# The start of a two-block transformer kernel reworked, one attention half reordered, and products of zeros put between hand-overs

## The reference

```
h += [stick_breaking(z), mlstm(z), spatial_gating(z)] @ w_out    # z = rms_norm(h, g1) @ w_in
h += moe(rms_norm(h, g2))                     # router: 4 groups of 8 experts, top 2
h += sigmoid(rms_norm(h) @ ple_gate) * (p @ ple_proj);   h = rms_norm(h)
h += (B * conv3(C * V)) @ sc_w_out            # [B|C|V] = rmsnorm(h) @ sc_w_in
h += conv_ffn(rmsnorm(h))                     # silu(g) * u @ w_down, 2816 wide
h += moba_attention(rmsnorm(h))               # 16 heads of 64, rope, causal softmax
h += conv_ffn(rmsnorm(h));  return rmsnorm(h)
```

## Time and profile before

| | |
|---|---|
| time, 3 runs | median 1277.6 us (1277.28 to 1283.98) |
| the profiled execution | 1279.39 us |
| its span | 1277.6 us |
| TensorE busy | 1174.7 us, 92% |
| VectorE busy | 864.5 us, 68% |
| ScalarE busy | 698.0 us, 55% |
| GpSimd busy | 124.3 us, 10% |
| mean granted TensorE clock | 0.957 |

### The profile page before, as it was taken

One profiled execution on the slowest core, in us unless ns is written; L12 is line 12 of the kernel. 1 busy time (PEld: TensorE's weight loads), 2 busy tenths in 40 slices (PEclk: granted clock), 3 DMA queues, 4 the chain that ended last, 5 costly groups with the idle time before them and its releaser, 6 DMA issues.

```text
span 1277.6 us, 18124 instructions
## 1 busy us (share of the span) xinstructions
PE 1174.7 (92%) x6806; PEld 1022.5 (80%) x6806; DVE 864.5 (68%) x1158; ACT 698.0 (55%) x961; POOL 124.3 (10%) x112
## 2 busy tenths in 40 slices
PE   6996767999999999997799989999999977999997
PEld 5885646788888888876599789999878766999996
DVE  5448576777877878775566566766676766666666
ACT  5368334666666667664453454555556655555453
POOL 0001120021200110200100011112000000111010
PEclk9996697999999999998999999999999988999999
DMA  7530133676777776774345435554443223445550
GB/s 309 178 119 1 52 145 114 220 291 251 269 276 255 270 287 239 286 279 147 129 166 201 165 139 192 193 193 175 158 175 122 100 100 116 158 177 192 197 197 33
DMA packets 32594, 232.09 MB, mean 182 GB/s; under 512 B 3616, under 2 KB 3616, under 8 KB 4768
## 3 DMA queue, kind: packets, MB, share of 16 engines
q1 hardware_dynamic: 32112, 230.08, 49.9%
q10 hardware_dynamic: 432, 1.31, 0.3%
HBM read 230.33 MB, written 1.05 MB: 181 GB/s over the span
## 4 chain that ended last, share of the span: by engine, by line
PE 82%; DVE 8%; ACT 6%; DMA 1%; issue 1%; POOL 1%; DVEq 0%; SPq 0%; ACTq 0%; POOLq 0%
PE bank L1646 16%; PE bank L1648 16%; PE bank L1647 16%; PE bank L1985 8%; PE bank L1986 8%; PE bank L1987 8%; DVE wlo L976 3%; PE bank L1875 2%; PE bank L1874 2%; DMA raw<-stream 1%; ACT whi L438 1%; ACT xn L452 1%; PE bank L1658 1%; ACT arena L802 1%; DVE arena L1441 1%
## 5 line engine op out<-in xcount | busy, mean ns | idle before, releaser
L976 DVE TENSOR_TENSOR wlo<-raw,whi 128x2048 fp32r<-128x2048 f32 x216 | 495.5, 2296 | 173.8 <-ACT whi L438 173.3
L438 ACT ACTIVATE whi<-raw 128x2048 fp32r<-128x2048 f32 x216 | 415.0, 1922 | 197.8 <-PE bank L1648 101.5
L1985 PE MATMUL bank<-xhi,whi 128*128 128x256 f32 x896 | 250.9, 280 | 4.9 <-DVE wlo L976 3.2
L1987 PE MATMUL bank<-xhi,wlo 128*128 128x256 f32 x896 | 250.4, 280 | 0.0
L1986 PE MATMUL bank<-xlo,whi 128*128 128x256 f32 x896 | 250.4, 280 | 0.0
L1646 PE MATMUL bank<-whi,rounded 128*128 128x512 f32 x600 | 243.4, 406 | 4.1 <-DVE rounded L1295 2.4
L1647 PE MATMUL bank<-wlo,rounded 128*128 128x512 f32 x600 | 239.2, 399 | 0.0
L1648 PE MATMUL bank<-whi,rounded 128*128 128x512 f32 x600 | 239.1, 398 | 0.0
L1985 PEld LDWEIGHTS bank<-xhi,whi 128*128 128x128 f32 x896 | 168.8, 188 | 6.9 <-DVE wlo L976 3.6
L1986 PEld LDWEIGHTS bank<-xlo,whi 128*128 128x128 f32 x896 | 168.7, 188 | 0.8
L1987 PEld LDWEIGHTS bank<-xhi,wlo 128*128 128x128 f32 x896 | 168.7, 188 | 0.0
(11 more groups left out here) (289 smaller groups left out, 1376.8 us busy)
## 6 DMA issues: line engine op xcount, KB each, us to landing
raw<-stream SPq DMA_DIRECT2D x216, 1024.0 KB, 4.8
xres<-x_in SPq DMA_DIRECT2D x1, 1024.0 KB, 5.0
arena<-finals ACTq DMA_DIRECT2D x2, 512.0 KB, 5.3
out<-xn SPq DMA_DIRECT2D x4, 256.0 KB, 2.6
par<-params SPq DMA_DIRECT2D x1, 876.0 KB, 9.6
cst<-table SPq DMA_DIRECT2D x1, 566.0 KB, 5.9
arena<-p_in ACTq DMA_DIRECT2D x1, 256.0 KB, 4.5
```

Source lines behind the costliest of these rows:

```text
L438: act.activation(whi[:, s, :], raw[:, s, :], ACT.Copy).then_inc(S("high_done"), 1)
L976: dve.tensor_tensor(wlo[:, s, :], raw[:, s, :], whi[:, s, :].bitcast(F32), ALU.subtract)\
L1985: pe.matmul(o, whi[:, s, w], xhi[:, kk, :], start=first, stop=False, skip_group_check=True)
L1987: ins = pe.matmul(o, wlo[:, s, w], xhi[:, kk, :], start=False, stop=kk == 7, skip_group_check=True)
```

## The change

Start: `x` is loaded in two tiles and unit 0 in four pieces; the identity and the gains come over ScalarE's DMA queue; the rest of the constants and parameters follow units 1 and 2. TensorE transposes `x` itself, not the normed `x`; the gain is multiplied in at `xhi` and `xlo`, which alternate with the pieces of unit 0, and `rstd` is multiplied in when `z` is copied out of its banks. ScalarE's squares come after the split of unit 0, before that of unit 1. The router weights are split later.

Zeros: `fill(n, b)` issues n matmuls of zeros, 512 columns each, into bank b, which nobody reads: 9 before `turn(0)`, 3 after; in `turn(2)` to `turn(7)` 7 (4 for q = 4) between tiles 0 and 1 and 3 after tile 1; 20 before the wait for `routed`.

`late`: in `add_chunks` at the short convolution's output and at the attention's output, VectorE splits the second unit of the next sublayer after `turn_dve`, not before the last adds.

Attention, second half: the last four heads' transposes of k (`turn_heads(3)`) come one product group earlier; VectorE splits the first output unit before `k_low`; `scores(8)` waits for three halves of q and k, not four; in the loop, `values` of head i-2 (not i-1) runs in iteration i, `turn_p` goes to its end, and ScalarE and VectorE do `pt_high` and `pt_low` of head i-2 first; the splits of the other output units move.

```diff
+            for t in range(TT):
+                sp.dma_start(xres[:, t, :], x_in[:, t, :]).then_inc(S(f"x{t}_loaded"), 16)
+            for k in range(4):
+                sp.dma_start(raw[:, 0, cols2(k)], stream[0][:, cols2(k)]).then_inc(S(f"piece{k}_landed"), 16)
+            sp.dma_start(raw[:, 1, :], stream[1]).then_inc(S("landed1"), 16)
+            sp.dma_start(cst[:, P:], table[:, P:]).then_inc(S("table_loaded"), 16)
+            sp.dma_start(raw[:, 2, :], stream[2]).then_inc(S("landed2"), 16)
+            sp.dma_start(par[:, GAINS:], params[:, GAINS:]).then_inc(S("params_loaded"), 16)
...
+            act.dma_start(cst[:, 0:P], table[:, 0:P]).then_inc(S("ident_loaded"), 16)
+            act.dma_start(par[:, 0:GAINS], params[:, 0:GAINS]).then_inc(S("gains_loaded"), 16)
+            act.wait_ge(S("gains_loaded"), 16)
+            for m in range(4):
+                act.wait_ge(S("turned"), m + 1)
+                for k in (2 * m, 2 * m + 1):
+                    ins = act.activation(xhi[:, k, :], turned_k(0, k), ACT.Copy, scale=Q("g0")[:, k:k + 1])
+                ins.then_inc(S("xhi_ready"), 1)
+                act.wait_ge(S(f"piece{m}_landed"), 16)
+                act.activation(whi[:, 0, cols2(m)], raw[:, 0, cols2(m)], ACT.Copy).then_inc(S("piece_high"), 1)
             norm_act(0)
-            split_to(0)
...
             split_to(1)
...
+                if c == 0:
+                    act.wait_ge(S("rstd0_ready"), 1)
+                act.activation(z[:, 0, 512 * c:512 * c + w], bank[2 * (c % 2)][:, 0:w], ACT.Copy, scale=rstd[:, 0:1])\
...
-            for i in range(9):
-                if i >= 1:
-                    pt_high(8 + i - 1)
+            for i in range(10):
+                if i >= 2:
+                    pt_high(8 + i - 2)
                 if i < 8:
                     weights(8 + i)
-                if i in (1, 5):
+                if i >= 3 and i % 2:
+                    o_high(4 + (i - 3) // 2)
+                if i in (2, 5):
                     split_to(U_WO + 2 + i // 4)
...
-                split_to(u0 + 5)
+                split_to(u0 + (4 if late else 5))
...
+            split_to(U_WO)
             k_low(1)
-            split_to(U_WO + 1)
             v_low(1)
-            for i in range(9):
-                head(8 + i, 8)
-                if i in (2, 6):
-                    split_to(U_WO + 2 + i // 4)
-                if i >= 2 and i % 2 == 0:
-                    o_low(4 + i // 2 - 1)
+            for i in range(10):
+                if i >= 2:
+                    pt_low(8 + i - 2)
+                if i < 8:
+                    maxima(8 + i)
+                    over_sums(8 + i)
+                if i in (1, 3, 6):
+                    split_to(U_WO + 1 + i // 3)
+                if i >= 3 and i % 2:
+                    o_low(4 + (i - 3) // 2)
...
+            def fill(n, b):
+                for _ in range(n):
+                    pe.matmul(bank[b][:], zeros_r[:], zeros_r[:].unsqueeze(1).broadcast_to([P, 4, P]), start=True,
+                              stop=True, skip_group_check=True)
+            FILL = {2: (7, 3, 2), 3: (7, 3, 4), 4: (4, 3, 2), 5: (7, 3, 2), 6: (7, 3, 4), 7: (7, 3, 2)}
             def turn(q):
                 for t in range(TT):
+                    if t and q in FILL:
+                        fill(FILL[q][0], FILL[q][2])
...
+                if q in FILL:
+                    fill(FILL[q][1], FILL[q][2])
...
+            fill(9, 0)
             turn(0)
+            fill(3, 0)
...
+            fill(20, 2)
             pe.wait_ge(S("routed"), 1)
...
-                pe.wait_ge(S("qk_ready"), 4 if h < 8 else 8)
+                pe.wait_ge(S("qk_ready"), (4 if h % 8 else 3) + (0 if h < 8 else 4))
...
-            for i in range(9):
+            for i in range(10):
                 if i < 8:
                     scores(8 + i)
-                if i >= 1:
-                    turn_p(8 + i - 1)
+                if i >= 2:
+                    values(8 + i - 2)
                 if i == 4:
                     pe.wait_ge(S("v_ready"), 2)
                 if i < 8:
                     o_part(i // 4, 0, (i % 4,))
                 else:
-                    o_part(0, 1, (0,))
-                if i >= 1:
-                    values(8 + i - 1)
+                    o_part(0, 1, (i - 8,))
+                if 1 <= i < 9:
+                    turn_p(8 + i - 1)
```

More of the change, by code:

```diff
@@ L109 @@
 A_FINAL = 3072
+GAINS = 8 * KD
 A_V = 2048
@@ L1026, in add_down @@
                 add(1, 1, 7)
-            dve.wait_ge(S("x_loaded"), 16)
-            for t in range(TT):
-                normed(0, t)
-            split_to(0)
-            dve.wait_ge(S("table_loaded"), 16)
-            dve.wait_ge(S("params_loaded"), 16)
-            turn_dve(0)
+            dve.wait_ge(S("gains_loaded"), 16)
+            for m in range(4):
+                dve.wait_ge(S("xhi_ready"), m + 1)
+                for k in (2 * m, 2 * m + 1):
+                    dve.scalar_tensor_tensor(xlo[:, k, :], turned_k(0, k), Q("g0")[:, k:k + 1],
+                                             xhi[:, k, :].bitcast(F32), ALU.mult, ALU.subtract)\
+                       .then_inc(S("xt_ready"), 1)
+                dve.wait_ge(S("piece_high"), m + 1)
+                dve.tensor_tensor(wlo[:, 0, cols2(m)], raw[:, 0, cols2(m)], whi[:, 0, cols2(m)].bitcast(F32),
+                                  ALU.subtract).then_inc(S("piece_low") if m < 3 else S("low_done"), 1)
+            done[0] = 1
             split_to(1)
-            dve.wait_ge(S("setup_high"), 1)
-            dve.tensor_tensor(rlo[:], router_w, rhi[:].bitcast(F32), ALU.subtract).then_inc(S("setup_low"), 1)
             strict = C("strict").unsqueeze(1)
@@ L1061, in _ @@
                 w = min(512, N_IN - 512 * c)
-                dve.tensor_copy(z[:, 1, 512 * c:512 * c + w], bank[2 * (c % 2) + 1][:, 0:w]).then_inc(S("dve_freed"), 1)
-                if c == 2:
+                if c == 0:
+                    dve.wait_ge(S("rstd1_ready"), 1)
+                dve.tensor_scalar(z[:, 1, 512 * c:512 * c + w], bank[2 * (c % 2) + 1][:, 0:w], rstd[:, 1:2], None,
+                                  ALU.mult).then_inc(S("dve_freed"), 1)
+                if c == 0:
+                    dve.wait_ge(S("table_loaded"), 16)
+                    dve.wait_ge(S("params_loaded"), 16)
+                    dve.wait_ge(S("setup_high"), 1)
+                    dve.tensor_tensor(rlo[:], router_w, rhi[:].bitcast(F32), ALU.subtract).then_inc(S("setup_low"), 1)
+                elif c == 2:
                     dve.wait_ge(S("heads_turned"), 2)
@@ L1421, in _ @@
                                   xhi[:, 2 * f:2 * f + 2, :].bitcast(F32), ALU.subtract).then_inc(S("sc_ready"), 1)
-            add_chunks(U_SCOUT, C_SCOUT, 5)
+            add_chunks(U_SCOUT, C_SCOUT, 5, late=True)
             def ffn_dve(layer, e, off, e0):
@@ L1693, in dense @@
                             wait_turned(q, 4 * u + k)
+                            if u0 + u == 0 and k < 3:
+                                pe.wait_ge(S("piece_low"), k + 1)
+                            elif u0 + u == 0:
+                                wait_unit(0)
                             for t in range(TT):
```

61 lines of the change are left out of this document (30 added, 31 removed).

## The result

The changed kernel takes 1286.6 us (median of 20 runs, 1284.4 to 1289.8) beside 1282.1 us of the kernel before (20 runs in the same rounds, 1277.3 to 1287.6): ratio 1.0036, 95% interval 1.0023 to 1.0049, so 4.6 us slower by the ratio, inside the 0.5% called no change. The forecast was 1283.2: a sum of +5.6 us on 1277.6, the median of three runs. The difference came out at +4.6, and the rest of the distance to 1286.6 is the base: the median of 20 runs of the kernel before is 1282.1. Between the two profiled executions the difference is +7.9 (spans 1285.5 and 1277.6), because that of the kernel before (1279.39) lies 2.7 us under its kernel's median and that of the changed kernel (1287.33) 0.8 us over. The clock says the same: 0.957 in the profile of before, but 0.952 on the mean of the 35 executions of that kernel beside experiments 1 to 4.

The account below looks back on a forecast made before the run. TensorE holds 82% of the chain of waits, so a microsecond counts only where TensorE waits or runs slowly. Terms -2.0 + 6.8 - 3.1 + 0 + 3.9 = +5.6 us on 1277.6 give 1283.2 us, range 1271 to 1290.

Parts of the forecast that it names:

- The forecast of no change that can be told: Whole kernel: a time from 1271.2 to 1284.0 us, within 0.5% of before, given a chance of 0.52.
- The start (-2.0): Start: early first product saves 2.75 us, but a 4 us wait for unit 1 halves the clock, costing 0.75.
- The zeros at the hand-overs (+6.8 for turn(2) to turn(6)): turn(2) to turn(6): zeros between tiles delay tile 1 by 0.7, 2.1, 1.3, 0.6 and 2.1 us; ends +3 and +9.
- it costs its time: Hand-overs: a zero product occupies TensorE like any 512-column product, in order, wherever tile 1 is ready; 0.23 or 0.44 us.
- `late` at turn(7) (-3.1): turn(7): tile 0 ready earlier, product 2.4 us earlier; shorter wait keeps the clock up, 0.7 more; ends 0 and -3.8.
- The router's zeros (0): Router: 20 zeros fit inside the 9.74 us wait, but 5.1 us stay empty, so no gain; other end -5.2 us.
- The heads (+3.9): Attention, second half: values(8) starts 3.7 us earlier, but values(8) to values(15) takes 36.2 us against 28.35; ends -3.7 and +10.
- each iteration is a closed ring over two engines: Heads, ScalarE and VectorE: pt_high, pt_low, maxima, exponential, reciprocal and scaling follow in order, 3.95 us per iteration.
- the 4 without and 6 with a split: Heads: distances between `values` of about 4 us without a split and near 6 with ScalarE's would show the forecast.
- rival 1: Router and start: zeros hold the clock up, -5.2 us and -1 us, giving 1277.0 us; chance alone 0.15.
- rival 2: Heads: two-head lag hides the ring, values(8) to values(15) stays 28.35 us, giving 1275.6 us; chance alone 0.17.
- rival 3: Attention: stalls of the ring take the clock to half for about three heads, +7 us, giving 1290 us; chance 0.15.

Follow-up runs that it names:

- experiment 1: The changed kernel without the zeros of turn(2) to turn(7), those at start and router kept: 1282.9 us, ratio 1.0018 to the kernel before.
- experiment 2: The changed kernel with the second half of attention in its old order: 1282.4 us, ratio 1.0008 to the kernel before.
- experiment 3: The kernel before with only the new start, including its 9 and 3 zeros: 1278.0 us, ratio 0.9967.
- experiment 4: The kernel before with only `late`, the late split in add_chunks at turn(5) and turn(7): 1278.6 us, ratio 0.9974.
- experiment 8: The changed kernel with the maxima ahead of `pt_low` on VectorE in heads 8 to 15: 1288.2 us, ratio 1.0050 to the kernel before.
- experiment 9: The changed kernel with `turn_p` ahead of the output group on TensorE: 1285.2 us, ratio 1.0039 to the kernel before.
- experiment 10: The changed kernel with `turn_p` ahead of the output group and the maxima ahead of `pt_low`: 1282.9 us, ratio 1.0014 to the kernel before.
- experiment 12: The kernel before with only the zeros of turn(2) to turn(7): 1285.8 us, ratio 1.0054.
- experiment 6: The kernel before with 40 zeros in the router's wait, twice the change's: 1282.1 us, ratio 1.0003.
- experiment 5: The kernel before with the new start alone, but ScalarE splits unit 1 ahead of the squares of norm 0: 1272.7 us, ratio 0.9937.
- experiment 7: The kernel before with only the early start of attention's second half, the head loops as before: 1278.0 us, ratio 0.9985.
- experiment 11: The kernel before with new start (unit 1 first), `late` and early heads with old loops; no zeros but the start's: 1268.6 us, ratio 0.9921.

## Why the prediction was right, and where it was not

In the profiles the 7.9 us come together so: start -0.1, turn(2) +0.5, router and experts +1.4, the late start of turn(3) +1.8, its zeros +1.8, turn(4) +1.7, turn(5) +0.3, turn(6) +0.6, heads +3.3, turn(7) -2.5, behind it -0.9. The forecast of no change that can be told was right, and +5.6 lies near +4.6. But the number is in part luck: turn(6) was priced 1.5 us too high and the start some 2 us too little, while the stall at turn(3) and the half clock in the expert stage were in no term.

**The start (-2.0): right in kind, too small.** Alone it gave 4.2 us (2.4 to 6.0 by the interval). Its profile went as forecast: first product at 9.65, unit 0 done at 15.5, a wait of 3.3 us, then half clock. The mis-sized pieces pull both ways. For the half clock I had allowed at most 8 products; in this profile it took 14 (6.9 us), about 3 us, so that turn(1) was reached only 0.13 us earlier than before. In the profiles of experiments 1, 2, 8, 9 and 10 the same stretch was 3.4 us long, and turn(1) was reached 0.9 to 3.0 us earlier. One profile of a start with such a wait is a sample, not a price. The whole gain I cannot place row by row; some 3 of the 4.2 us lie in where the two profiled executions stand among the runs of their kernels.

**The zeros at the hand-overs (+6.8 for turn(2) to turn(6)): right in kind, too large.** Place by place, first transpose to first product after and before: turn(2) 4.48 for 3.97, +0.5 (forecast +0.7); turn(3) 5.69 for 3.93, +1.8 (+2.1); turn(4) 5.72 for 4.02, +1.7 (+1.3); turn(5) 4.46 for 3.60 less 0.6 of wait, +0.3 (+0.6); turn(6) 4.47 for 3.84, +0.6 (+2.1): 4.9 in all, and 4.3 for the same five in experiment 12. The mis-sized term is turn(6), to which I gave turn(3)'s half clock; it ran at 1.00 throughout, and so did turn(3) in experiment 12 (+0.6). In experiments 8, 9 and 10 turn(6) did fall into a stretch of half clock and took 6.06 us, +2.2 where I had forecast +2.1: the price of a zero, 0.23 or 0.44 us, hangs on when the clock falls. What fills the sum in the profile is a thing I had not seen: TensorE's stall at turn(3), an idle time of 4.50 us for 2.70 of before, +1.8 (against the time at which `xn` was ready the start is 3.1 us later). The larger error is in the rule "it costs its time". It holds on the kernel before (6.9 us). In the changed kernel taking all the zeros out gave back 2.3 us only, while the mean clock fell from 0.957 to 0.952. The term leaves out that zeros can hold the clock up in other stages; in the profile of experiment 1 the heads took 2.9 us more at half clock. Why the zeros do this in the changed kernel and hardly on the kernel before, no run shows.

**`late` at turn(7) (-3.1): right.** In the profile, from the last product before it to the first behind it 5.90 us, for 8.43 before: -2.5 (forecast -2.4), and behind it the distance shrinks by 0.9 more (forecast 0.7 by the clock). Alone `late` gave 3.3 (1.2 to 5.5).

**The router's zeros (0): right, with half the reason.** The gathers did stand at 0.50 behind the 5.07 us that stayed empty. But experiment 6 shows that filling it doesn't bring the 4 to 5 us either: the clock then falls inside the gathers, and in its profile what they gain is spent behind them. The other end of that term, -5.2, was not to be had by zeros. In the profile of the change the half clock lasts until 212.5, not 209.5, and from the router's first product to the end of the experts it is 413.94 us for 412.55.

**The heads (+3.9): right in size, wrong in mechanism.** values(8) came 4.2 us earlier relative to turn(6) (forecast 3.7), the stretch behind took 35.9 us (forecast 36.2), and the old order gave 3.6 us back. The step that failed is "each iteration is a closed ring over two engines". The ring that held was one over three: `values`, output group, `turn_p`, `pt_high`, `pt_low`. It takes about 4 us at full clock, 5.3 in the iteration of the chain at half, nearly what mine takes, and the split terms were the same for both; so a wrong path gave a right number by luck. From one `values` to the next the changed kernel takes 5.5, 5.4, 5.3, 6.4, 4.5, 4.9 and 3.9 us, not the 4 without and 6 with a split that I gave as signs. I didn't see the path in time, and only the exchange that should have opened it (experiment 8) told. I had followed the order on ScalarE and VectorE instruction by instruction, and read TensorE's new order only for what it starts, not for what waits behind what.

**The rivals.** The zeros as holders of the clock (rival 1): at the start the first 24 products did run at 1.00 (before, nine at 0.44 us), but the next wait undid it; at the router no; at the hand-overs in part, by the mean clocks of experiment 1. The Trainium skill, "TensorE: Matmul & The Clock Gate", Part 4, by which transposes don't count for the clock, would have had the zeros of turn(3) pay for themselves; in experiment 12 turn(3) takes 4.49 us where it took 3.93, and the kernel is 6.9 us slower. Transposes alone did raise the clock, at turn(4) of the kernel before (shown at the end). The heads running apart (rival 2): no order with a lag of two heads came to the 28.35 us. Half clock in the heads (rival 3): two stretches of 3.4 us in the changed kernel, 17 us in experiment 1; it is a real mechanism, and it comes and goes between kernels whose heads are alike.

## What to carry to other kernels

A filler on an in-order engine costs its full time at its place wherever what comes behind it is already ready: before adding one, find the hand-overs where the second tile is ready when the first is done, and leave those out. When a loop is reordered across several in-order queues, write down for each queue what now stands ahead of what, and look for every closed path, the one through the busiest engine first; opening one shows only when it was the longest. A short wait that appears behind an early start is worth more than its length, because the clock goes with it; look for what stands ahead of the late unit and is not needed yet (3.8 us here for one exchanged line). And before a place is priced by the half clock that one profile shows there, compare the mean clocks of all executions of both kernels.

## What the runs showed of the hardware

The clock fell while TensorE was busy: in experiment 6 from 1.00 to 0.50 at 198.5, 2.3 us into back-to-back gathers of 128 columns that each load their own weights. Whether the gathers or the pause of 1.17 us ahead of them let it fall, no run tells apart.

Transposes alone can raise the clock. At turn(4) of the kernel before TensorE stands idle for 9.09 us until 636.59 and then does 16 transposes and nothing else until 639.98; the granted clock goes from 0.50 to 1.00 at 639.5. A window over the 16:

```profile
636.59:639.98 3.39, 3.39 (x16) 2.99 (x16) 1.25 (x4) 0.94 (x3) 0.98 (x2) 0.57 0.00 0
```

At turn(3) TensorE stands still in some kernels for no reason that the profile shows. The idle time before the first transpose (2.70 us before, 4.50 in the change, 1.23 in experiment 1) doesn't tell it, since it also holds the ordinary wait for `xn`. The distance from VectorE's start on `xn` to the first transpose does: it is 0.54 us before,

```profile
594.79 0.89 DVE L987 TENSOR_SCALAR xn<-xres,rstd 128x512 f32<-128x512 f32 x2 [0.66 <-POOL rstd L877]
```

where the first transpose starts at 595.33, and 0.53 or 0.54 in experiments 1, 3, 4, 5, 7, 11 and 12; it is 3.65 in the change (595.26 to 598.91) and 3.72 to 3.98 in experiments 2, 8, 9 and 10. In experiment 6 the stall comes four transposes later:

```profile
595.09 1.12 PE L1666 MATMUL bank<-cst,xn 128*128 128x128 f32 x4 [2.69 <-DVE xn L989]
598.20 2.82 PE L1666 MATMUL bank<-cst,xn 128*128 128x128 f32 x12 [1.99 <-issue]
```

Just ahead of turn(3) the program branches past the overflow code, and in all six kernels with the stall it ends 2.2 to 2.5 us after a packet of the queue of kind "instruction". So I take it for the loading of code at a place that moves with the program's length. The Trainium skill, "Runtime: NRT & Kernel Launch", section "Instruction fetch mechanics", says that a taken branch beyond what is loaded stalls until it is fetched. The rows agree with it only in part: TensorE loads its first weights behind the branch at 595.80 and stalls after that, and the kernels without a stall have such a packet in the same stretch as well. No run moved the code alone, so the cause is argued, not shown. It is worth 2.0 to 3.4 us: as much as most edits of this change.
